# Loading the first keys of two cache attentions ahead of their phases, in memory that the attention phases share

## What is computed

```python
def dilated_window_sample(q, k, v, buf_k, buf_v, bias_tab):      # B, samples
    kc = jnp.concatenate([buf_k, k], axis=1)                     # 2048 old keys + 8 new ones
    ...
    logit = einsum('nthe,ntjhe->nthj', q, kg) + bias; p = exp(logit - max); out = p @ v / sum(p)

def dsa_sample(q, k, v, qx, kx, wx, pool_k, pool_v, pool_idx, page_table, layer, bias_tab):   # C, samples
    _, idx = lax.top_k(indexer_scores(...), ksel)
    kg = pool_k[phys, layer, off]                                # gathered by the page table
    return gathered_softmax(q, kg, vg, q_pos - idx, bias_tab)
```

## Time and profile before

| | |
|---|---|
| time, median of 3 runs | 2843.06 us (2836.44 to 2845.73) |
| profiled execution, its own time | 2844.74 us |
| span of its trace (first to last instruction) | 2843.0 us |
| PE, matmuls | 2527.0 us busy, 89% of the span |
| DVE / ACT / POOL | 1375.8 / 707.1 / 539.7 us busy |
| mean granted TensorE clock | 0.939 of full |
| read and written in HBM | 262 MB and 68 MB, 116 GB/s over the span |

### The profile page before, as it was taken

The page is one execution under the profiler, slowest core; times in us unless marked ns, Lnnn a source line. Parts: engine busy times, 40 slices in busy tenths (PEclk is TensorE's granted clock), DMA queues, the critical chain, the costliest instruction groups (busy, mean ns, idle before and its releaser), DMA issues. The chain is left out here.

```text
span 2843.0 us, 35054 instructions
## 1 busy us (share of the span) xinstructions
PE 2527.0 (89%) x13940; PEld 1742.8 (61%) x13940; DVE 1375.8 (48%) x2324; ACT 707.1 (25%) x1387; POOL 539.7 (19%) x535
## 2 busy tenths in 40 slices
PE   6999999584789997787868769999999998999998
PEld 4555544242577877455545435688888887888743
DVE  0589999352467665486724213422222224444333
ACT  3222220042344544575513200111111110000011
POOL 2000000102444431400036601122222220000000
PEclk9999999685799999798979979999999999999999
DMA  7111111612244542611989953101111114020211
GB/s 269 49 43 37 48 36 40 194 37 79 92 133 152 160 134 88 203 47 63 356 284 352 359 211 111 41 30 45 45 45 35 40 45 144 2 82 1 85 37 36
DMA packets 148459, 305.15 MB, mean 107 GB/s; under 512 B 49784, under 2 KB 99128, under 8 KB 146010
## 3 DMA queue, kind: packets, MB, share of 16 engines
q1 hardware_dynamic: 115986, 169.65, 18.6%
q0 software_dynamic: 25904, 98.19, 9.2%
q10 hardware_dynamic: 6408, 35.08, 3.8%
HBM read 262.23 MB, written 67.77 MB: 116 GB/s over the span
## 5 line engine op out<-in xcount | busy, mean ns | idle before, releaser
L482 PE MATMUL i_psM<-i_w,i_xnT 128*128 128x462 f32 (+2 forms) x1152 | 422.5, 525 | 2.3 <-ACT i_xnT L312 2.3
L482 PEld LDWEIGHTS i_psM<-i_w,i_xnT 128*128 128x128 f32 x1152 | 218.6, 192 | 194.4 <-issue 174.1
L1261 PE MATMUL m_B<-m_big,m_arena 128*128 128x272 f32 x1408 | 328.4, 394 | 4.0 <-DVE m_actT L1004 3.2
L1261 PEld LDWEIGHTS m_B<-m_big,m_arena 128*128 128x128 f32 x1408 | 268.4, 191 | 59.9 <-DVE m_actT L1004 3.4
L1261 PE MATMUL m_B<-m_arena 128*128 128x272 f32 x1056 | 245.6, 392 | 0.0
L1261 PEld LDWEIGHTS m_B<-m_arena 128*128 128x128 f32 x1056 | 200.6, 190 | 41.4
L894 POOL TENSOR_TENSOR m_arena<-m_arena 128x512 f32<-128x512 f32 x110 | 138.1, 1288 | 400.2 <-DMA m_arena<-w_gate 198.1
L1295 PE MATMUL m_B<-m_arena 128*128 128x256 f32 x880 | 193.1, 382 | 8.9 <-DVE m_arena L1053 8.9
L1295 PEld LDWEIGHTS m_B<-m_arena 128*128 128x128 f32 x880 | 168.1, 191 | 33.5 <-issue 6.6
L1078 DVE TENSOR_TENSOR m_actT<-m_actT,m_B 128x544 f32<-128x544 f32 x88 | 60.6, 719 | 198.9 <-PE m_B L1261 198.9
L1078 DVE TENSOR_TENSOR m_arena<-m_arena,m_B 128x544 f32<-128x544 f32 x88 | 60.4, 719 | 193.1 <-PE m_B L1261 192.9
(11 more groups left out here) (427 smaller groups left out, 3935.4 us busy)
## 6 DMA issues: line engine op xcount, KB each, us to landing
b_Kp<-b_k SPq DMA_DIRECT2D x32, 512.0 KB, 11.4
b_Vp<-b_v SPq DMA_DIRECT2D x32, 512.0 KB, 14.1
o_bk<-b_k ACTq DMA_DIRECT2D x8, 2040.0 KB
o_bv<-b_v ACTq DMA_DIRECT2D x8, 2040.0 KB
m_arena<-w_gate SPq DMA_DIRECT2D x11, 1024.0 KB, 5.4
m_arena<-w_up SPq DMA_DIRECT2D x11, 1024.0 KB, 5.3
m_arena<-w_down SPq DMA_DIRECT2D x8, 1408.0 KB, 8.2
i_w<-w_in POOLq DMA_DIRECT2D x5, 1848.0 KB, 34.6
```

Of the source, the lines that this page charges most:

```text
L482: mm = nc.tensor.matmul(psM[:, q % 2, 0:cols.stop - cols.start], xnT[:, t % RING, k, :], w[:, k, cols], start=(k == 0), stop=(k == KO - 1))
L1261: mm = nc.tensor.matmul(B[:, 2 * (q % pairs.SLOTS) + b, 0:QUARTER], stationary(s, m)[:, k, :], moving[m][:, k, b * QUARTER:(b + 1) * QUARTER],
```

## The change

- **Shared memory.** A class `Early` holds one arena of 16,896 floats per partition, `ident` and its semaphore for all attention blocks and mlp. The 8 key slots, the transposed keys and `Qb` lie in it (class `Samples`), and so do the prompt's `prob`, `PT` and `out`, which share addresses with the transposed keys and `Qb`, not with the key slots. The prompt's `rows`, `outT` and `flip` lie in two tiles of the search that are first used in its last steps. mlp takes the same arena and `ident`.
- **Prompt to b.** In the prompt's SP queue, after the last rows (tile 7) and ahead of the store of tile 4, 13 DMAs are added: b's new rows, page numbers and part, two masks, and b's first 8 key pieces.
- **b to c.** DVE computes c's piece numbers in b, ahead of the chunk loop (9 instructions). SP loads c's new rows in b after all of b's pieces. POOL, after the selection has been stored, waits for b's value piece 27 (the last but four), and then issues c's first 8 key pieces.
- **c** starts its SP queue with `spread`, `unsel` and the new values; `load_pieces` skips the first 8 keys in both blocks.
- **mlp** has no load of `ident` and no wait for it.
- Attend and mlp become parts of one phase `rest`, each with a clean-up, around which lies one more clean-up, with its barrier, at the end of the program.

```diff
@@ phase_prompt, sync
                     if i + 2 < QT:
                         sp.wait_ge(S["rowsT"], NG * (i + 1))
                         load(i + 2)
+                    if i == QT - 3:
+                        samples.load_new(sp, D, COL_B)
+                        samples.load_small(sp, D)
+                        for k in range(samples.KS):
+                            samples.load_key(sp, D, "b", k)
                     if i:
                         store(i - 1)
@@ phase_sample
                 def keys(numbers):
                     for k in numbers:
                         if k >= KS:
                             eng.wait_ge(S["keysT"], 2 * (k - KS + 1))
-                        piece_dma(eng, "c_k" if sparse else "b_k", k, Kp[:, k % KS, :], K_in[k % KS])
+                            samples.load_key(eng, D, tag, k)
...
                 if sparse:
-                    sp.dma_start(pages[:, :], D["pages"]).then_inc(idx_in, 16)
-                    sp.dma_start(part[:, :], D["sub"]).then_inc(idx_in, 16)
-                    load_small(sp)
-                    load_late(sp)
+                    sp.dma_start(spread[:, :, :], D["spread"]).then_inc(spread_in, 16)
+                    for k in range(2):
+                        sp.dma_start(unsel[64 * k:64 * k + 64, :], D["s_unsel"]).then_inc(unsel_in, 16)
+                    load_vnew(sp)
                 else:
                     load_pieces(sp)
+                    sp.wait_ge(turned, 1)
+                    samples.load_new(sp, D, COL_C)
...
                     pool.wait_ge(s_unsel_out, 48)
+                    pool.wait_ge(samples.idx_at, 1 + PAST // P // 4)
+                    v = 4 * CH - 5
+                    pool.wait_ge(V_in[v % VS], 16 * (v // VS + 1))
+                    for k in range(KS):
+                        pool.wait_ge(S["keysT"], 2 * (4 * CH - KS + k + 1))
+                        samples.load_key(pool, D, "c", k)
@@ class Samples (new)
+        self.Kp = early.arena[:, 0:8192].rearrange("p (s w) -> p s w", s=self.KS)
+        self.KpT = early.arena[:, 8192:16384].rearrange("p (u n i w) -> p u n i w", u=2, n=4, i=2)
+        self.Qb = early.arena[:, 16384:16896].rearrange("p (i n w) -> p i n w", i=2, n=N_SEQ)
@@ phase_mlp, sync and tensor
-                sp.dma_start(ident[:, :], D["ident"]).then_inc(ident_in, 16)
...
-                pe.wait_ge(ident_in, 16)
@@ (new)
+def phase_rest(nc, D):
+    with ExitStack() as ctx:
+        early = Early(nc, ctx)
+        with nc.cleanup_on_exit():
+            phase_attend(nc, D, early)
+        with nc.cleanup_on_exit():
+            phase_mlp(nc, D, early)
```

More of the change, by code:

```diff
@@ L619, in step_end, with phase_mlp @@
         return (s + 1) * len(self.ORDER)
-def phase_mlp(nc, D):
+def phase_mlp(nc, D, early):
     LIVE = SEQ + 64
@@ L654, in phase_mlp @@
         junk = sb("junk", [P, D_MODEL])
-        ident = sb("ident", [P, P])
+        ident = early.ident
         gffn = sb("gffn", [P, KO])
@@ L2529, in phase_prompt @@
         sem = lambda n: nc.alloc_semaphore("p_" + n)
-        ident = sb("ident", [P, P])
+        ident = early.ident
         identb = sb("identb", [P, P], BF16)
-        flip = sb("flip", [P, P])
         bias = sb("bias", [P, 8, SPAN])
-        rows = sb("rows", [P, 2, 2, 2 * B_W])
+        rows = kth.rank[:, 0:2048].rearrange("p (u i w) -> p u i w", u=2, i=2)
+        outT = kth.same[:, 0:256].rearrange("p (r w) -> p r w", r=2)
+        flip = kth.same[:, 256:256 + P]
         KT = sb("KT", [P, 4, SEQ])
@@ L2537, in phase_prompt @@
         QTt = sb("QTt", [P, 2, 4, P])
[L2538 to L2539 removed]
+        prob = early.arena[:, 8192:12288].rearrange("p (m u w) -> p m u w", m=2, u=2)
+        PT = early.arena[:, 12288:16384].rearrange("p (m u j w) -> p m u j w", m=2, u=2, j=QT)
+        out = early.arena[:, 16384:16896].rearrange("p (k w) -> p k w", k=2)
         unsel = sb("unsel", [P, 2, SEQ], BF16)
@@ L2551, in phase_prompt @@
         S = {n: sem(n) for n in (
-            "consts identb rowsT rows_out logits logit nmx prob probT PT pv outT rden own").split()}
+            "identb rowsT rows_out logits logit nmx prob probT PT pv outT rden own").split()}
         rows_in = [sem(f"rows_in{u}") for u in range(2)]
@@ L2585, in _ @@
                     sp.dma_start(bias[:, h, :], src).then_inc(table_in[h], 16)
-                sp.dma_start(ident[:, :], D["ident"]).then_inc(S["consts"], 16)
+                sp.dma_start(ident[:, :], D["ident"]).then_inc(early.ident_in, 16)
                 def load(i):
@@ L2874, in phase_sample @@
         sem = lambda n: nc.alloc_semaphore(f"{tag}_" + n)
[L2875 to L2878, removed]
+        ident, hmask, pick, new = early.ident, samples.hmask, samples.pick, samples.new
+        Qb, Kp, KpT = samples.Qb, samples.Kp, samples.KpT
         vnew = sb("vnew", [DEC, N_SEQ, B_W])
-        Qb = sb("Qb", [P, 2, N_SEQ, 32])
         KnT = sb("KnT", [P, 2, 64])
@@ L2913, in phase_sample, with load_vnew @@
         keysT_out = [sem(f"keysT_out{i}") for i in range(2)]
-        K_in = [sem(f"K_in{n}") for n in range(KS)]
+        K_in = samples.K_in[tag]
         V_in = [sem(f"V_in{n}") for n in range(VS)]
-        def source(name, g, c, n):
-            return D[name][4 * g + n].rearrange("(p j) w -> p j w", j=J)[:, 4 * c:4 * c + 4, :]
         with nc.Block() as block:
[L2921 to L2931, removed]
+            def load_vnew(eng):
                 eng.dma_start(vnew[:, :, :], D["proj"][SEQ:SEQ + 64, COL + 2 * B_W:COL + 3 * B_W]
                               .rearrange("(n t) w -> t n w", t=DEC)).then_inc(vnew_in, 16)
[L2935 to L2944, removed]
             def load_pieces(eng):
@@ L3101, in finish @@
                     dve.wait_ge(S["out_new"], g + 1)
-                    if g == 0:
-                        dve.wait_ge(masks_in, 32)
+                    if g == 0 and not sparse:
+                        dve.wait_ge(samples.masks_in, 32)
                     nc.vector.scalar_tensor_tensor(on[:, :], B[:, 6, 0:B_W], rden[:, g:g + 1], hmask[:, :], ALU.mult,
@@ L3133, in _ @@
                         .then_inc(turned_out, 1)
+                if not sparse:
+                    piece_numbers()
                 for ch in range(CH):
@@ L3485, in phase_attend @@
+def phase_attend(nc, D, early):
     with ExitStack() as outer:
         far = Relative(nc, outer, "c", PAST, 4)
+        samples = Samples(nc, outer, early)
         with ExitStack() as ctx:
```

100 lines of the change are left out of this document (65 added, 35 removed).

## The result

After the change the kernel takes 2824.48 us (median of 6 runs, 2820.37 to 2828.17), against 2841.89 us before (6 runs, 2836.44 to 2845.73): ratio 0.9938 with an interval of 0.9927 to 0.9950, 17.4 us faster. The forecast was 2821.3 with a range of 2812 to 2833 and "faster" at 0.86. The profiled execution took 2823.86 us, its span 2822.1.

A forecast was written before the change was run, and what follows sets the result against it. It took b to be paced by transfers, with poor stretches at block starts and ends where PE waits for late-requested data. Terms -10.2, 0, -13.5, +1.0, -0.4, +1.3 sum to -21.8 from 2843.06: 2821.3 us, range 2812 to 2833.

The forecast's parts named there:

- the rival that the border waits: Border from b to c: the final store waits for all eight early pieces, price 5.0 us, total 2825.3; chance 0.13.
- b's pieces in the prompt: Block b: first 8 key pieces and new rows loaded in the prompt make b's transfers 8 pieces shorter, -10.2 us.
- the plateau's own number: Block b: 8 pieces at 1.28 us each, the pace of uninterrupted transfers at 409 GB/s, give 10.2 us.
- The price in the prompt: Prompt: 13 more DMAs delay tile 4's stores, but 14 us of cover before ACT needs them makes the cost 0.
- slower: Prompt: early loads hold SP's queue past 27 us, stopping ACT and then PE, total 2851.3 us; chance 0.04.
- c's pieces and numbers: Block c: first 8 key pieces loaded at b's end and the chain of numbers gone from c's start, -13.5 us.
- the transfer number: Block c: gain counted from transfers, 10.2 for fewer pieces, 1.4 and 3.1 for the start, together 14.7 us.
- c late: Border: POOL is held, so c's pieces do not start before it; 13.0 us gained, total 2830.1; chance 0.12.
- the slots eat it: Blocks b and c: full slots idle the DMA engines until PE has worked; 8.0 us gained, 2835.1; chance 0.09.
- The border: From b to c: last value pieces and final store each fall about half a piece behind, +1.0 us, upper end +5.0.
- `ident` of mlp: Start of mlp: SP no longer issues the load that PE's start hangs behind, -0.4 us.
- The clean-up: Program end after mlp: one extra clean-up and barrier that nothing hides, +1.3 us, ends 0 and 1.3.

The follow-up runs named there:

- e3: Changed kernel with neither early load: b's new rows and first keys loaded in b, c's keys in c; 2836.67 us, ratio 0.9981.
- e1: Changed kernel without the border loads: c's first eight key pieces issued at c's start, b's still loaded in the prompt; 2827.34 us, ratio 0.9947.
- e4: Changed kernel with four of c's key pieces loaded at b's end instead of eight, the other four at c's start; 2826.71 us, ratio 0.9940.
- e10: Changed kernel with PE's mask wait after the second chunk's transposes, b's stores waited for in c, outer clean-up serving as mlp's; 2821.83 us, ratio 0.9923.
- e13: e10 with six of c's key pieces loaded at the border instead of eight; 2823.80 us, ratio 0.9941.
- e11: e1 plus one indirect load of one piece issued by POOL at b's end, to a slot nobody reads; 2827.63 us, run once.
- e12: e1 plus one plain load of a b key piece, same size, issued by POOL at b's end; 2833.09 us, run once.
- e9: Changed kernel in which b no longer waits for its output stores; c waits for them instead; 2824.52 us, ratio 0.9941.

## Why the prediction was right, and where not

The direction and the two blocks were right, and the size within 4.4 of 17.4; the sum of -21.8 was too large, because the border's price was put too low and c's gain too high. The time itself, 2824.48, is nearer to the rival that the border waits (2825.3, chance 0.13) than to the forecast of 2821.3 (0.62).

*b's pieces in the prompt, -10.2:* -9.85 by the profiles of e3 and e1, 9.3 by their medians. The profiles understate it: b's last value chunk took 1.93 in e3 at a granted clock of 1.00 and 3.23 in e1 at 0.58, and up to that chunk the difference is 11.15. So the term is good to one or two us, not to the 0.35 that the two numbers suggest. The steps held: new rows at once, DVE's first search step at T+2.87 (forecast T+3.0, with the piece numbers ahead of it), the next key chunk at T+12.2 without a DMA wait. What did not hold is the reason "the plateau's own number": behind the start the engines moved 351 GB/s, not 409, and the wait for keys came back as 6.8 us in all (9.2 before).

*The price in the prompt, 0:* held. The eight keys were issued in 4.63, tile 4's first store went at 1247.56, that store landed 9.7 later at 1257.3, as forecast, and ACT wrote tile 5 of that kind at 1267.39 without a wait for it, so 10.1 us of the cover of 14 were there. The stretch moved 322 GB/s beside the usual work. The rival "slower" is not borne out.

*c's pieces and numbers, -13.5:* -11.9. This term was mis-sized, and by one choice: "nearer to the transfer number" (14.7), where PE's number (11.5) carried it. I had PE's path right to 0.2 (third chunk's start forecast at T+14.2, measured T+14.41), with two small misses that partly cancel: the mask came at T+8.4 in place of T+8.1, and the second chunk with its products took 5.98 in place of 6.1 (my own row gave 5.94). The first four pieces took 5.77 in place of 7, which changed nothing, since the mask came last. That e3 kept 5.6 of the gain without any early piece, where the rival "c late" counts 3.7, I had not seen. After that start c lasts 177.0 to 180.3 us in every run, whatever was loaded early: 205.40 - 25.73 = 179.7 before, 193.47 - 14.41 = 179.1 after, 199.47 - 22.43 = 177.0 in e1, 198.78 - 19.08 = 179.7 in e4, 191.27 - 12.59 = 178.7 in e10, 195.22 - 16.44 = 178.8 in e13. With early pieces of c it is 178.7 to 180.3, without them (before, e1, e3, e11, e12) 177.0 to 179.7, so what the transfers saved ahead of this point gives nothing behind it; the DMA engines pause instead (347 GB/s where it was 405). In this the rival "the slots eat it" was partly right, for c, and its sign, below 300 GB/s in the first 15 us, is there in c with 276 and not in b with 336.

*The border, +1.0:* this step failed. The border itself costs 2.9 to 4.0 (4.42 and 5.54 against 1.57), and b as a whole 2.7 to 4.8 more, part of it the clock. The upper end of 5.0 and the rival were near in size, and the sign that I named for it (over 3 us between store and c) is there with 4.42. My reason against it, that few loads would stand in the queue because POOL's pace of 1.24 is not faster than the transfers' 1.28, was no reason at all: 1.24 is the shorter of the two, and it is the landing of the last load that counts, not the queue. The rule of the Trainium skill that I weighed (DMA: Bandwidth & Descriptors, Queues, rings and completion order) is that a DMA's semaphore write lands only after the earlier writes of its DMA engine. The trace agrees in that the store was late behind the loads, 4.2 to 4.6 us to landing in place of 1.5. It does not bear out what I had made of the rule, a store that waits for all eight pieces: in e9 the store landed 1.0 ahead of a load that was issued before it, in e10 0.7. And the store is not what holds the border, since e9 without that wait is as late. The price was found by the right row, 7.5 us to landing, and put down to the wrong waiter.

*`ident` of mlp, -0.4:* +0.1, nothing. *The clean-up, +1.3:* +0.4 (4.00 in place of 3.60; 3.56 in e10 without it), nearer to the lower end, as its one semaphore suggested.

The terms as measured: -9.85 - 11.9 + 3.8 + 0.1 + 0.4 = -17.5, against -17.4 in the medians. That they meet to 0.1 is chance: each term comes from one profile of each kernel, each of the two terms of b holds 1.3 us of clock, and b of e3 is 0.36 longer than b of before. The forecast was also counted from 2843.06, while before was 2841.89 over all its runs; by luck this makes the time miss by 3.2 where the gain missed by 4.4.

## What to carry to other kernels

Loads issued ahead over a border are worth what the first consumer can start earlier; read that from the timeline of that engine, and take no second gain from the transfers unless they still decide where the two paths meet. A load of POOL in flight at the border had its own price here, the landing of the last one less the moment when the block would have ended, even though nobody in the block waits for it. So move loads far ahead, as b's in the prompt, for which no profile shows a price; where slots come free only at the end, weigh that price against the consumer's wait, piece by piece.

## What the runs showed that I had not expected

A block's end waited for the DMAs that POOL had issued, though no instruction there waited on their semaphores: c's start came 0.4 to 0.8 us behind the landing of the last load in nine profiles, and one load of 512 KB lengthened the border from 1.57 to 4.59 (plain) and 5.36 us (indirect). No row names the instruction that waits, and whether it is POOL's queue alone, or any engine's, was not tried. The stretch at the lower clock fell on b's last matmuls in some executions and ahead of them in others, 1.3 us at the very end of the path, and b's last value chunk began up to 2.9 us apart with nothing changed ahead of it, so that b's length alone, from one profile, doesn't settle an effect of one or two us.
